# Weights of the attention made half a step earlier, groups ending in second half steps, RWKV projections summed by token blocks

## The reference, cut to what matters

```python
u = _rms_norm(x, norm_mix[l]) @ w_in[l]
q, kc, vc, ks, vs, kw, vw, nsa_gl, rw, merge = _split(u, IN_SPLITS)
o_nsa = _nsa(q, kc, vc, ks, vs, kw, vw, nsa_gl, ...)      # sum over branches: gate * softmax(q k) v
o_rwkv, v_first = _rwkv7(rw, v_first, vres, ...)          # shift, low ranks, recurrence, norm, gate
gates = sigmoid(merge).reshape(B, S, 2, D)
y = gates[:, :, 0] * (o_nsa @ proj_nsa[l]) + gates[:, :, 1] * (o_rwkv @ proj_rwkv[l])
x = x + y @ w_out[l]
```

## Time and profile before

| | |
|---|---|
| median of 3 runs | 1651.03 us (1648.91 to 1651.04) |
| profiled execution | 1647.32 us, of which the span is 1645.6 us |
| TensorE busy | 1610.9 us (98%) |
| VectorE, ScalarE, GpSimd busy | 1010.1, 884.4, 133.2 us |
| mean granted clock of TensorE | 0.995 of full speed |
| delta net, mixer | about 680 to 965 us, about 1178 to 1448 us of the span |

### The profile page before, as it was taken

How to read it: one execution, slowest core, us unless ns; L and a number is a source line. 1 busy time by engine, 2 the same in 40 slices (tenths; PEclk the granted TensorE clock), 3 DMA queues, 4 the chain that set the end, 5 groups by cost and what they waited for, 6 DMA issues and landing times.

```text
span 1645.6 us, 25757 instructions
## 1 busy us (share of the span) xinstructions
PE 1610.9 (98%) x10213; PEld 1323.8 (80%) x10213; DVE 1010.1 (61%) x1572; ACT 884.4 (54%) x1376; POOL 133.2 (8%) x152
## 2 busy tenths in 40 slices
PE   8999999999999999999999999999998899999999
PEld 7888888888888888877887878888876687788887
DVE  5555565755556554687676676554666645766673
ACT  6454465645455543785555555443676533466662
POOL 2000001000000000204020010000210000002220
PEclk9999999999999999999999999999999999999999
DMA  8666565666557655542222458655532212456652
GB/s 275 190 181 191 179 205 166 205 184 187 190 165 217 183 187 175 193 152 80 90 79 82 125 167 229 183 189 166 178 120 89 78 31 90 153 175 183 177 181 90
DMA packets 209240, 261.76 MB, mean 159 GB/s; under 512 B 21803, under 2 KB 145122, under 8 KB 209122
## 3 DMA queue, kind: packets, MB, share of 16 engines
q1 hardware_dynamic: 208834, 259.60, 51.4%
q10 hardware_dynamic: 288, 0.52, 0.1%
HBM read 259.01 MB, written 1.05 MB: 158 GB/s over the span
## 4 chain that ended last, share of the span: by engine, by line
PE 86%; DVE 7%; ACT 4%; issue 1%; POOL 1%; DVEq 0%; ACTq 0%
PE acc L459 25%; PE acc L461 24%; PE acc L460 24%; DVE low L434 2%; PE tr L717 1%; ACT high L424 1%; PE aux L1004 1%; PE tr L535 1%; PE tr L3477 1%; DVE gdn_cv L1454 1%; PE aux L1012 1%; PE aux L2728 1%; PE aux L1019 0%; PE acc L3075 0%; DVE gdn_kf L1385 0%
## 5 line engine op out<-in xcount | busy, mean ns | idle before, releaser
L434 DVE TENSOR_TENSOR low<-raw,high 128x1024 fp32r<-128x1024 f32 (+1 forms) x488 | 590.3, 1225 | 402.1 <-ACT high L424 401.2
L424 ACT ACTIVATE high<-raw 128x1024 fp32r<-128x1024 f32 (+1 forms) x488 | 503.8, 1047 | 354.1 <-PE acc L461 344.3
L459 PE MATMUL acc<-high,xh 128*128 128x512 f32 (+1 forms) x1344 | 540.3, 402 | 4.4 <-DVE low L434 2.9
L461 PE MATMUL acc<-high,xl 128*128 128x512 f32 (+1 forms) x1344 | 523.2, 389 | 0.0
L460 PE MATMUL acc<-low,xh 128*128 128x512 f32 (+1 forms) x1344 | 521.7, 388 | 0.0
L459 PEld LDWEIGHTS acc<-high,xh 128*128 128x128 f32 x1344 | 253.5, 189 | 59.0 <-issue 6.2
L461 PEld LDWEIGHTS acc<-high,xl 128*128 128x128 f32 x1344 | 253.2, 188 | 53.5
L460 PEld LDWEIGHTS acc<-low,xh 128*128 128x128 f32 x1344 | 254.1, 189 | 46.9 <-issue 0.7
L459 PE MATMUL acc<-high,hh 128*128 128x512 f32 x472 | 185.7, 393 | 0.0
L461 PE MATMUL acc<-high,hl 128*128 128x512 f32 x472 | 183.9, 390 | 0.0
L460 PE MATMUL acc<-low,hh 128*128 128x512 f32 x472 | 183.7, 389 | 0.0
(11 more groups left out here) (472 smaller groups left out, 1656.2 us busy)
## 6 DMA issues: line engine op xcount, KB each, us to landing
raw<-in_ffn_w_gate_up SPq DMA_DIRECT2D x350, 256.0 KB, 3.2
raw<-in_ffn_w_down SPq DMA_DIRECT2D x176, 256.0 KB, 3.0
raw<-in_gdn_w_in SPq DMA_DIRECT2D x96, 256.0 KB, 3.0
raw<-in_ffn_up SPq DMA_DIRECT2D x88, 256.0 KB, 3.2
raw<-in_w_in SPq DMA_DIRECT2D x72, 256.0 KB, 2.9
raw<-in_sc_w_in SPq DMA_DIRECT2D x48, 256.0 KB, 3.2
raw<-in_ffn_down SPq DMA_DIRECT2D x44, 256.0 KB, 3.0
raw<-in_gdn_w_out SPq DMA_DIRECT2D x32, 256.0 KB, 3.0
```

What stands on the lines that cost most here:

```text
L424: nc.scalar.activation(high[t % HIGHS][:, 0:n], raw[t % RAWS][:, 0:n], ACT.Copy).then_inc(high_ready, 1)
L434: nc.vector.tensor_tensor(low[t % RAWS][:, 0:n], raw[t % RAWS][:, 0:n], high[t % HIGHS][:, 0:n].bitcast(F32), ALU.subtract).then_inc(low_r ...
L459: nc.tensor.matmul(o, a, wh, start=(k0 + kk == 0), stop=False)
L461: mm = nc.tensor.matmul(o, b, wh, start=False, stop=(k0 + kk == k - 1))
```

## The change

1. Weights u+1 of the attention are made in the second half of step u (`weights_dve`), with weights 0 in the first half of step 0, ahead of the compressed branch's coefficient. In step 7 their places are taken by `keys_dve` and `bonus_keys_dve`, which stood at the head of `rwkv_dve`.
2. Two fill steps come earlier (third core step 5 for 4, fourth 2 for 1), two later ones go (the first half of step 7, the second RWKV step), so that groups end in second halves.
3. The turn of the value columns 8 and 9 stands before the two `krb` turns, in the time of GpSimd's root; `rinv` has a place of its own.
4. The low half of the attention output is made by VectorE in the inverse's step 8, its high half two steps earlier (`i == 7`).
5. The RWKV projection is run by token blocks: four tiles for block 0, then four for block 1; gates and sums follow block by block. The gates of `pn + 1` stand between the two halves of the RWKV output's gating.
6. In the delta net VectorE's taps 6 and 7 are next to each other, norms go one place later each, norms 7 behind the grams; `key_factors_dve` stands one step later.

`MIX_ORDER` follows (left out below).

```diff
@@ GatedDelta.dve
-                for s, n in self.TAIL:
-                    if s < 8:
-                        self.taps_dve(dve, s)
-                    self.norms_dve(dve, s - 2)
-                    self.some(fill, n)
+                n6, n7, n8, n9 = (n for _, n in self.TAIL)
+                self.taps_dve(dve, 6)
+                self.taps_dve(dve, 7)
+                self.norms_dve(dve, 4)
+                self.some(fill, n6 + n7)
+                self.norms_dve(dve, 5)
+                self.some(fill, n8)
+                self.norms_dve(dve, 6)
+                self.some(fill, n9)
                 self.grams_dve(dve, 0)
+                self.norms_dve(dve, 7)
                 self.some(fill, self.FIRST)
...
@@ GatedDelta.other_dve
                     self.scores_dve(dve, 0)
                     yield
-                    self.key_factors_dve(dve)
                     yield
                 for h in range(2):
                     if R >= 2:
                         self.turn_dve(dve, R - 2, h)
+                    if R == 0 and h == 0:
+                        self.key_factors_dve(dve)
...
@@ Mixer
-            NSA = ((1, 0), (2, 0), (4, 0), (1, 0)) + 7 * ((2, 1), (2, 1)) + ((1, 0), (1, 0), (1, 0))
-            RWKV = (2, 2, 1, 1, 1, 1) + 8 * (0,) + 3 * (1,) + 10 * (1,) + (0, 3, 4, 3, 0)
+            NSA = ((1, 0), (2, 0), (5, 0), (2, 0)) + 7 * ((2, 1), (2, 1)) + ((0, 0), (1, 0), (1, 0))
+            RWKV = (2, 1, 1, 1, 1, 1) + 8 * (0,) + 3 * (1,) + 10 * (1,) + (0, 3, 4, 3, 0)
...
@@ Mixer.fill_pe, fill_dve, gated, both_dve (the last two now for one token block each)
-                pe.wait_ge(self.PL.sem, self.PL.at["on_low"])
+                pe.wait_ge(self.DV.sem, self.DV.at["on_low"])
...
-                        if t == tiles_of[gi][-1]:
-                            self.gated(dve, gi, j)
+                        if j == 0 and t == tiles_of[gi][-1]:
+                            for tb in range(TB):
+                                self.gated(dve, gi, 0, tb)
...
@@ Mixer.pe
-                pe.wait_ge(DV.sem, DV.at["or_low", 1])
-                products(pe, self.pr, self.orh, self.orl)
-                products(pe, self.pr + 1, self.orh, self.orl, at_=1, then=first_two)
+                ts = tiles_of[self.pr] + tiles_of[self.pr + 1]
+                for tb in range(TB):
+                    pe.wait_ge(DV.sem, DV.at["or_low", tb])
+                    for t in ts:
+                        if tb and t == ts[-1]:
+                            first_two()
+                        tile_products(pe, t, tb, self.orh, self.orl)
...
@@ Mixer.dve
+                low_to(dve, tiles_of[self.pr][0] + AHEAD)
+                for j in range(2):
+                    self.gated(dve, self.pr + j, 2 + j, 0)
+                    self.both_dve(dve, j, 0)
+                self.gated(dve, self.pr, 2, 1)
+                self.both_dve(dve, 0, 1)
                 stream_dve(dve, self.pr)
-                self.gated(dve, self.pr, 2)
-                self.both_dve(dve, 0)
-                low_to(dve, tiles_of[self.pr + 1][0] + AHEAD)
                 y_low(0)
                 y_low(1)
-                stream_dve(dve, self.pr + 1)
-                self.gated(dve, self.pr + 1, 3)
-                self.both_dve(dve, 1)
+                self.gated(dve, self.pr + 1, 3, 1)
+                self.both_dve(dve, 1, 1)
...
@@ Mixer.nsa_dve
                     if u < 7:
                         self.masked(dve, u + 1)
+                    else:
+                        self.keys_dve(dve)
                     if u == 0:
+                        self.weights_dve(dve, 0)
...
-                    dve.wait_ge(AC.sem, AC.at["ex", u, 1, 1])
-                    nc.vector.reciprocal(self.inv_[:, u % 2, :], self.sm[:, u % 2, :]).then_inc(DV.sem, DV.one(("inv", u)))
...
+                    yield
+                    if u < 7:
+                        self.weights_dve(dve, u + 1)
+                    else:
+                        self.bonus_keys_dve(dve)
                     yield
...
@@ Mixer.side_pe (side_act: shift 8 two steps earlier; side_dve: shifts 8 and 10 one and two steps earlier)
+                pe.wait_ge(DV.sem, DV.at["kmx"])
+                self.side_turn(pe, 3, 0)
+                yield
                 for h in range(2):
-                    pe.wait_ge(DV.sem, DV.at["kkn", 0] if h else DV.at["krnx"])
+                    if h:
+                        pe.wait_ge(DV.sem, DV.at["kkn", 0])
+                    else:
+                        pe.wait_ge(DV.sem, DV.at["shifted", 8])
+                        pe.wait_ge(DV.sem, DV.at["krnx"])
...
@@ Mixer.rwkv_act, rwkv_dve, rwkv_pool
-                    if i == 9:
+                    if i == 7:
                         act.wait_ge(PE.sem, PE.at["RK", 1])
...
+                    if i == 8:
+                        dve.wait_ge(AC.sem, AC.at["on_high"])
+                        nc.vector.tensor_tensor(self.onl[:, :, :], self.on[:, :, :], self.onh[:, :, :].bitcast(F32),
+                                                ALU.subtract).then_inc(DV.sem, DV.one("on_low"))
...
                 self.gated_dve(dve, 1)
+                for tb in range(TB):
+                    self.gated(dve, self.pn + 1, 1, tb)
                 self.or_low_dve(dve, 1)
...
-                pool.wait_ge(AC.sem, AC.at["on_high"])
-                m.tensor_tensor(self.onl[:, :, :], self.on[:, :, :], self.onh[:, :, :].bitcast(F32), ALU.subtract).then_inc(PL.sem, PL.one("on_low"))
```

More of the change, by code:

```diff
@@ L137 @@
         ("shift", 2), ("shift", 3), "kksq", ("PTc", 4, 0), ("PTb", 4), ("PTc", 4, 1), ("PT", 4), ("on", 0),
-        "icw", ("ex", 6, 0, 0), ("ex", 6, 0, 1), ("ex", 6, 1, 0), ("ex", 6, 1, 1), ("PTc", 5, 0), ("PTb", 5),
-        ("PTc", 5, 1), ("PT", 5), ("ex", 7, 0, 0), ("ex", 7, 0, 1), ("ex", 7, 1, 0), ("ex", 7, 1, 1),
-        ("shift", 8), ("shift", 9), ("PTc", 6, 0), ("PTb", 6), ("PTc", 6, 1), ("PT", 6), ("shift", 10),
+        "icw", ("ex", 6, 0, 0), ("ex", 6, 0, 1), ("ex", 6, 1, 0), ("ex", 6, 1, 1), ("shift", 8), ("shift", 9),
+        ("PTc", 5, 0), ("PTb", 5), ("PTc", 5, 1), ("PT", 5), ("ex", 7, 0, 0), ("ex", 7, 0, 1),
+        ("ex", 7, 1, 0), ("ex", 7, 1, 1), ("PTc", 6, 0), ("PTb", 6), ("PTc", 6, 1), ("PT", 6), ("shift", 10),
         ("shift", 11), ("PTc", 7, 0), ("PTb", 7), ("PTc", 7, 1), ("PT", 7), ("on", 1), ("g", 0), ("g", 1),
@@ L152 @@
         ("nm", 0, 0, 1), ("nm", 0, 1, 0), ("nm", 0, 1, 1), "csum", "c01", ("sm", 1, 0), ("sm", 1, 1),
[22 rows of a table removed]
-        ("ycen", 0), ("SA", 3), ("ysqs", 0), ("yvar", 0), ("yn", 0), ("yb", 1), ("ysum", 1), ("ymean", 1),
-        ("ycen", 1), ("ybon", 0), ("or", 0), ("ysqs", 1), ("yvar", 1), ("yn", 1), ("or_low", 0), ("ybon", 1),
-        ("or", 1), ("or_low", 1), ("y", 0, 0), ("y", 0), ("y", 1, 0), ("y", 1),
[23 rows of a table added]
+        ("ymean", 1), ("ycen", 1), ("ybon", 0), ("or", 0), ("ysqs", 1), ("yvar", 1), ("yn", 1), ("or_low", 0),
+        ("ybon", 1), ("or", 1), ("or_low", 1), ("y", 0, 0), ("y", 1, 0), ("y", 0), ("y", 1),
     ],
@@ L181 @@
         ("cm", 0.0), "masks", "krn", ("v", 0, 0), ("v", 0, 1), ("v", 1, 0), "v", "kcrn", "cinv", "kkrn",
-        "on_low", ("yrn", 0), ("yrn", 1),
+        ("yrn", 0), ("yrn", 1),
     ],
@@ L2236, in __init__ @@
                 self.krn = c("mix_krn", [16])
+                self.rinv = c("rw_rinv", [16])
                 self.vc = c("mix_vc", [P])
@@ L2395, in gate, with gated, both_dve @@
                 return work[:, tb, g * GW:(g + 1) * GW] if g < 2 else prod[g - 2][tb][:, :]
[L2397 to L2404, removed]
-                DV = self.DV
[L2406 to L2410, removed]
+            def gated(self, dve, gi, g, tb):
+                dve.wait_ge(acc_ready[tb], gi + 1)
+                wait_left(dve, self.merge + g, tb)
+                o = self.gate(g, tb)
+                nc.vector.tensor_tensor(o, at_acc(gi, tb)[:, :], o, ALU.mult).then_inc(left(gi, tb), 1)
+            def both_dve(self, dve, j, tb):
+                DV = self.DV
+                wait_left(dve, self.pn + j, tb)
+                wait_left(dve, self.pr + j, tb)
+                o = self.gate(j, tb)
+                nc.vector.tensor_tensor(o, o, self.gate(2 + j, tb), ALU.add).then_inc(DV.sem, DV.one(("y", j, tb) if tb == 0 else ("y", j)))
             def pe(self, pe, nxt):
@@ L2854, in nsa_dve @@
                         nc.vector.tensor_tensor(cs, cs, self.ccoef[:, :, :].unsqueeze(3).broadcast_to(m), ALU.mult).then_inc(DV.sem, DV.one("Pc"))
-                    dve.wait_ge(AC.sem, AC.at["ex", u, 1, 1])
-                    nc.vector.reciprocal(self.inv_[:, u % 2, :], self.sm[:, u % 2, :]).then_inc(DV.sem, DV.one(("inv", u)))
-                    dve.wait_ge(DV.sem, DV.at["inv", u])
-                    nc.vector.tensor_tensor(self.coef[:, u % 2, :].rearrange("p (b t) -> p b t", b=2),
-                                                   self.inv_[:, u % 2, :].rearrange("p (b t) -> p b t", b=2),
```

(36 more changed lines are left out.)

10 lines of the change are left out of this document (2 added, 8 removed), and 47 rows, old and new, of the table MIX_ORDER.

## The result

The changed kernel takes 1628.49 us (median of 4 executions, 1628.19 to 1628.88) against 1651.03 for the kernel before (median of 4, 1648.91 to 1651.68): a ratio (of the means) of 0.9866, with a 95% interval of 0.9854 to 0.9878. That is 22.5 us less, where 15.1 were forecast.

What follows compares the result with a forecast made beforehand. TensorE, busy for 98% of the span, was taken as the bound, leaving its waits and lower clock to gain. The terms 2.0 + 8.4 + 1.0 + 3.7 = 15.1 us off 1651.0 gave 1635.9, said as 1636, range 1629 to 1643.

Steps and rivals of the forecast that it cites:

- Delta net: VectorE's new order of taps, norms and key factors shortens TensorE's waits for taps and decay products; 2.0 us gained.
- Low half of the attention output: Made on VectorE instead of GpSimd, it removes TensorE's wait at the inverse's end; 1.0 us gained.
- Token blocks: RWKV projections: the 2.0 us wait for the low half and the 1.7 us slow stretch go; 3.7 us gained.
- Attention: Weights half a step ahead remove the transposes' waits; 10.9 us of new waits and clock loss against 19.3; 8.4 gained.
- The start: Start of the attention: filler halves delay the compressed weights' sum; TensorE waits 3.4 us where it was 0.9, plus 1.7 clock.
- the receptance turn: Attention, turn of the receptance columns: ScalarE's copies, table load and exps pile up; a wait of 1.6 us.
- the norms' broadcast: Attention: GpSimd's root of 3.8 us is mostly covered by the turn of the value columns; a wait of 0.9 us.
- the last values behind the merge gate: Attention: the gate's table load and sigmoids stand ahead of shift 10 and the last probability copies; 1.7 us wait.
- The median: Base of the sum: the gain is taken from the three runs' median 1651.0, 3.7 us above the profiled execution.
- B: Rival, attention: waits at the start and before the last values don't come; 5.9 us better, 1630 us; chance 0.15.
- C: Rival, attention: ScalarE's list becomes the bound and TensorE waits at side turns instead; 1642 us; chance 0.20.
- E: Rival, attention: VectorE's list becomes the bound and the kernel slower; about 1658 us at 15 us a step; chance 0.04.

Runs made afterwards that it cites:

- the version with the weights alone: Changed kernel with all the attention's other edits taken back and only the weights left half a step ahead; 1633.73 us.
- three repairs of the start wait: Changed kernel with the sixth fill product early (1625.54 us), with sum and first weights early (1625.62), or with these and the tanh early (1625.53).
- no blocks: Changed kernel with the RWKV projections tile by tile again, both token blocks of a tile together; 1631.41 us.
- the kernel without the onl part: Changed kernel with the low half of the attention output made by GpSimd again, its high half two steps later on ScalarE; 1629.72 us.
- before, again: The kernel before, unchanged, timed and traced again; median 1650.85 us, profiled execution 1652.02 us.
- weights and tables: Changed kernel with the attention's side steps and the place of the key products as before, weights and fill tables kept as changed; 1633.46 us.

## Why the prediction was off

**Delta net, 2.0 forecast.** 2.04 between the traces, +2.5 by its experiment. TensorE waits 0.6 at the grams (0.4 said) and 0.2 at the inverse (0.4 said). Right.

**Low half of the attention output, 1.0.** 1.06 and +1.2. Right.

**Token blocks, 3.7.** 3.5 and +2.9. The wait of 2.0 is gone; the turn of `y`, which I had at no wait, costs 0.2. Right, with the clock's part coming in some executions and not in all.

**Attention, 8.4.** This is the first of two steps that failed: 12.2 between the traces, +17.1 by the experiment. The step is the list of waits that come out when the transposes' waits go. The start was as walked through (3.2 us against 3.4, with its slow stretch), and so were the tanh (1.2 against 1.0) and short ones. The walk's own numbers give 1217.5 - 1214.2 = 3.3 there. Too dear were the receptance turn (1.1 against 1.6), the norms' broadcast (0.3 against 0.9), and the last values behind the merge gate (0.6 against 1.7). In all TensorE idles 6.9 in the stretch where I had 9.2. On the other side I had 14.1 of idle time, to 1310 us; the wait of 0.7 for the bonus products at 1310.5, which also went, lay outside that window. These two make 2.3 + 0.5 = 2.8 of the missing 3.8. For the last 1.0, busy time beyond what the windows of the clock explain, I have no row; its cause stays open.

**The median** is the second step that failed: "It is 3.7 us under the median of the three runs shown, 1651.0; I take the difference from that median." The clock losses in the sum, 5.2 + 1.7, were those of a fast execution. The one traced again, at 1652.02, has 8.5 + 1.7, and it has them where they cost time: it is 4.7 us longer. No execution at the median itself was traced; that the 3.7 us of the median are of this kind follows from its mean clock (0.994, where the fast group has 0.996) and is not shown directly. The change takes away the waits behind which the stretches come, so this slow time went too. I had read from one trace that a wait of 2.0 or more is followed by a stretch of 1.7 and one of 1.8 is not; the runs show none, one or two of them behind long waits, and single ones behind waits of 1.8 and 1.1. With this the executions also draw together: the four of the changed kernel take 1628.2 to 1628.9, where those of the kernel before reach from 1647.1 to 1653.2.

The attention was 3.8 us too low and the median 3.7, of a miss of 7.5 (1636 against 1628.5). With either of the two right I would have said about 1632, and with the same width of 7 us to either side 1628.5 lies inside; it took both to leave the range.

**The rivals.** B (the waits at the start and before the last values don't come) gave the nearest time, 1630, but its mechanism is half right: the one before the last values shrank to 0.6, the one at the start came in full. C and E did not happen: ScalarE held TensorE for 1.2 and 0.6 us, and for 1.1 at the receptance turn. That wait is put down to VectorE's shift, but VectorE stood 2.18 us for ScalarE's high half ahead of it, behind the table load, the exp and the exps of the scores that the prediction names:

```profile
1250.68 1.23 DVE L434 TENSOR_TENSOR low<-raw,high 128x1024 fp32r<-128x1024 f32 x1 [2.18 <-ACT high L424]
1252.74 0.66 PE L2909 MATMUL tr<-ident,prod 128*128 128x128 f32 x4 [1.10 <-DVE mix_rwf L3031]
```

E's price was also added up wrongly: at 15 us a step, 7.5 steps take 112.5 us, 16.5 more than 96; less 6.7 that is 9.8 over the median, 1661 and not 1658. C's mechanism is the one of the version with the weights alone, which my count of the fill products as "moved, not added: +1, +1, -1 and -1, so their time cancels" passed over: their time cancels, but where a group ends does not.

**The table load.** The load ahead of the last values is 1.28 us long with the function starting right behind (1285.03 + 1.28, next at 1286.33), and the last values waited 0.6. The rule of the Trainium skill (ScalarE: Activation LUTs, What ACT_TABLE_LOAD costs), 2.66 us with its drain, would have made that wait longer yet; the trace decides against it here.

## What to carry to other kernels

Before subtracting from a median, ask which execution was profiled: where waits of 2 us stand close together, a median execution can hold more slow time than the trace, and a change that removes the waits gives this back too. The mean clock alone understates this (0.995 against 0.994 here), because a slow stretch where TensorE is not the bound lowers it and costs nothing; a second trace, compared at the same instructions, tells more. When an engine's queue is reordered so that the bound engine arrives earlier, walk the places where it hands over buffers (here the end of a fill group) as well as those where it takes data: a fill table that was harmless at the old pace brought 6 us of waits at the new one, and the changed kernel with it is 2.7 us slower. And a wait that is cut by more than the next one in line can follow moves on: three repairs of the start wait, worth 4.5 to 4.9 us on paper, each gave 2.9 to 3.0.

## What the runs showed of the hardware

How long the clock stays low behind a wait, in the profiled executions, from their windows. Behind the start wait of 3.2 us it was 1.7 us of loss in three kernels, 3.4 in two, and nothing in one (no blocks); in the fastest execution of the kernel without the onl part, with that wait in its program, the mean clock is 1.000. Behind a wait of 2.9 for `prod` it was 1.7 in both kernels that have it, but nothing behind the second, of 2.6 and 2.8; behind one of 1.9 once 1.7 and once nothing; in the variants of the changed kernel, behind 1.8 and below nothing. The kernels with the old attention had one behind a wait of 0.7, among narrow products, in two traces of three, one behind 1.8 (the kernel with the attention undone) and one behind 1.1 (before, again), and other waits of 1.8 without any. The longest, in the kernel with weights and tables:

```profile
1212.00:1216.00 4.00, 0.81 (x6) 0.79 0.45 135
1216.00:1220.00 4.00, 4.00 (x14) 0.50 0.00 0
1220.00:1224.00 4.00, 2.83 (x13) 0.85 0.22 55
```

A granted clock of 0.50 is 1.2 GHz for the whole window. What decides between none, one and two lengths, these runs do not show.
